# Sample attention of a decoder step: keys of two pairs before values of two pairs, values in 64-column tiles, probability copies moved between engines

## What is computed

```
comp  = compressed blocks of the past                     # 32 of them
p_c   = softmax(q @ comp.K - slope * distance)            # importance of blocks
idx   = top 16 blocks by sum of p_c over the group's heads
o_s   = softmax(q @ K[idx] - slope * distance) @ V[idx]   # selected branch
o_w   = softmax(q @ Kwin  - slope * distance) @ Vwin      # window of 512
o     = gate0 * p_c @ comp.V + gate1 * o_s + gate2 * o_w
```

## Time and profile before

| what | value |
|---|---|
| median of three runs | 909.55 us |
| the profiled execution's own time | 906.55 us |
| span of that execution | 904.7 us |
| sample stage in the span | 310.4 to 417.4 us |
| TensorE busy over the span | 826.2 us (91%) |
| VectorE, ScalarE, GpSimd busy | 418.0, 335.7, 135.0 us |
| mean granted TensorE clock | 0.96 of full speed |

### The profile page before, as it was taken

How to read it: one execution, slowest core, us unless ns; L and a number is a source line. 1 busy time by engine, 2 the same in 40 slices (tenths; PEclk the granted TensorE clock), 3 DMA queues, 4 the chain that set the end, 5 groups by cost and what they waited for, 6 DMA issues and landing times.

```text
span 904.7 us, 18157 instructions
## 1 busy us (share of the span) xinstructions
PE 826.2 (91%) x7775; PEld 752.2 (83%) x7775; DVE 418.0 (46%) x782; ACT 335.7 (37%) x626; POOL 135.0 (15%) x160
## 2 busy tenths in 40 slices
PE   5999998997888867785999999999999999999995
PEld 4999977775555645465999999999999999999995
DVE  5435646664555475565327433344233433243432
ACT  6511155552566565463225431133212331043311
POOL 0001101100785345530220000000000000000120
PEclk9999999998899889896999999999999999999998
DMA  8912628842461206526221122222221122222002
GB/s 299 323 72 95 192 70 248 259 168 93 134 206 36 83 1 233 190 79 178 94 93 50 48 89 93 93 93 93 93 86 41 59 93 93 94 93 93 1 1 105
DMA packets 48794, 103.03 MB, mean 114 GB/s; under 512 B 7499, under 2 KB 19167, under 8 KB 46430
## 3 DMA queue, kind: packets, MB, share of 16 engines
q1 hardware_dynamic: 41821, 68.61, 23.1%
q0 software_dynamic: 6912, 33.56, 10.9%
HBM read 97.75 MB, written 8.53 MB: 117 GB/s over the span
## 4 chain that ended last, share of the span: by engine, by line
PE 52%; DVE 1%; ACT 0%; DVEq 0%; issue 0%
PE banks L2003 51%; PE banks L2044 0%; DVE y L1993 0%; PE banks L2070 0%; DVE wl L1923 0%; PE banks L2060 0%; ACT wh L1867 0%; DVE hT L1936 0%; DVE hT L1961 0%; DVE xl L1940 0%; ACT low L1881 0%; DVE xl L1929 0%; ACT xh L1883 0%; DVEq L1816 0%; ACT small L1911 0%
## 5 line engine op out<-in xcount | busy, mean ns | idle before, releaser
L2003 PE MATMUL banks<-xh,wh 128*128 128x288 f32 x640 | 138.3, 298 | 4.3 <-DVE xl L1929 3.9
L2003 PE MATMUL banks<-xl,wh 128*128 128x288 f32 x640 | 138.1, 297 | 0.0
L2003 PE MATMUL banks<-xh,wl 128*128 128x288 f32 x640 | 137.7, 297 | 0.0
L1867 ACT ACTIVATE wh<-low 128x1024 fp32r<-128x1024 f32 x72 | 75.0, 1050 | 103.1 <-PE banks L2003 102.9
L2003 PE MATMUL banks<-ah,wh 128*128 128x288 f32 x512 | 110.2, 297 | 0.0
L2003 PE MATMUL banks<-al,wh 128*128 128x288 f32 x512 | 109.6, 296 | 0.0
L2003 PE MATMUL banks<-ah,wl 128*128 128x288 f32 x512 | 109.6, 296 | 0.0
L2003 PEld LDWEIGHTS banks<-xh,wh 128*128 128x128 f32 x640 | 104.0, 190 | 5.0 <-DVE wl L1923 4.2
L2003 PEld LDWEIGHTS banks<-xl,wh 128*128 128x128 f32 x640 | 104.1, 190 | 0.0
L2003 PEld LDWEIGHTS banks<-xh,wl 128*128 128x128 f32 x640 | 104.0, 190 | 0.0
L1961 DVE TENSOR_TENSOR hT<-banks,hT 128x288 f32<-128x288 f32 x64 | 26.3, 453 | 138.9 <-PE banks L2003 138.9
(11 more groups left out here) (340 smaller groups left out, 1372.3 us busy)
## 6 DMA issues: line engine op xcount, KB each, us to landing
low<-in_w_up SPq DMA_DIRECT2D x8, 2048.0 KB, 8.2
low<-in_w_down SPq DMA_DIRECT2D x8, 2048.0 KB, 7.7
zone<-in_cmp_w SPq DMA_DIRECT2D x16, 256.0 KB
o_swin<-in_state_win SPq DMA_DIRECT2D x8, 504.0 KB
px<-in_x_prompt SPq DMA_DIRECT2D x4, 512.0 KB, 5.3
u_raw<-in_w_in SPq DMA_DIRECT2D x1, 2048.0 KB, 10.0
q_raw<-in_w_in SPq DMA_DIRECT2D x1, 2048.0 KB, 10.4
low<-in_state_win SPq DMA_DIRECT2D x4, 512.0 KB
```

The lines of the kernel that those rows point to most:

```text
L1867: act.activation(wcols(m.wh, i), raw_cols(i), ACT.Copy).then_inc(wh_ready, 1)
L2003: last = pe.matmul(out(i, hf), w[wi], half(x[:, k, :], hf), start=first and part == 0, stop=end and part == 2)
```

## The change

- TensorE's program becomes phases of two pairs: K0 K1 V0 V1 K2 K3 V2 V3. V1 and K2 change places. `turn_output` of a pair b-1 stands behind K(b), with `small_scores` waiting for one more stored output (`o_kept`).
- `values` uses two matmuls a position tile instead of four: 64 probability columns of one e (both groups) stationary, 128 value columns of both groups moving. Half of the results (probabilities of one group with values of the other) are computed and not used. The merge reads the full 128 columns.
- For pairs 0 and 2 ScalarE copies all six units of turned probabilities; for pairs 1 and 3 the split of three and three stays.
- ScalarE's queue: `exponents(b)` stands behind `keep_keys` of units 0 to 3 of pair b+1; `exponents(b+1)` stands behind all six copies of pair b.
- VectorE's queue: scores of b, scores of b+1, merge of b, its copies of b+1, merge of b+1.
- GpSimd issues all page loads of pair 2, then all of pair 3, in a row behind the bias of pair 1, each waiting for the unit whose slot it fills.

The diff, cut to its core:

```diff
+    COPIER = [(("act",) * VN, ("act",) * 3 + ("dve",) * 3)[n % 2] for n in range(NPAIR)]
+    def keep_probs(eng, n, i):
+        eng.wait_ge(p_turned, VN * n + i + 1)
+        if VN * n + i >= 3:
+            eng.wait_ge(v_done, VN * n + i - 2)
...
-                if 1 <= n < NPAIR - 1:
-                    for i, x in enumerate(ORDER):
+                if n == 1:
+                    for b in range(2):
+                        for i, x in enumerate(ORDER):
+                            if x < 4:
+                                pool.wait_ge(v_done, VN * b + i + 1)
+                                for e in range(2):
+                                    load_pages(pool, m, b + 2, e, x, sems)
...
+            for b in range(0, NPAIR, 2):
+                for u in range(3):
+                    pack(act, b, u)
+                keys_of(b, 0, UN)
+                if b:
+                    keep_output(b - 1)
+                for u in range(3):
+                    pack(act, b + 1, u)
+                keys_of(b + 1, 0, 4)
+                exponents(b)
+                keys_of(b + 1, 4, UN)
+                for i in range(VN):
+                    keep_probs(act, b, i)
+                exponents(b + 1)
+                for i in range(VN):
+                    if COPIER[b + 1][i] == "act":
+                        keep_probs(act, b + 1, i)
+                keep_output(b)
...
+            for b in range(0, NPAIR, 2):
+                scores_of(b)
+                scores_of(b + 1)
+                merge(b)
+                for i in range(VN):
+                    if COPIER[b + 1][i] == "dve":
+                        keep_probs(dve, b + 1, i)
+                merge(b + 1)
...
             def small_scores(n):
-                if n >= 3:
-                    pe.wait_ge(o_kept, n - 2)
+                if n >= 2:
+                    pe.wait_ge(o_kept, n - 1)
...
+                out = lambda e, r: pb[4][64 * e:64 * e + 64, P * r:P * r + P]
                 for mm in range(QUAD if i < X else 0):
-                    for e, g in tiles:
+                    for e in range(2):
+                        last = pe.matmul(out(e, int(ORDER[i] == 4)).rearrange("p (g d) -> p g d", g=NKV),
+                                         m.spT[i % 3][:, P * mm + 64 * e:P * mm + 64 * e + 64],
+                                         m.slot[2 * (n % 2) + e][:, ORDER[i], mm, :]
+                                         .rearrange("p (g k) -> p g k", g=NKV)[:, :, HD:2 * HD],
+                                         start=(i == 0 and mm == 0), stop=False, skip_group_check=True)
...
+            for b in range(0, NPAIR, 2):
+                keys_of(b)
+                if b:
+                    pe.wait_ge(sel_step, b * SEL_STEPS + 1)
+                    turn_output(b - 1)
+                keys_of(b + 1)
+                values_of(b)
+                values_of(b + 1)
             turn_output(NPAIR - 1)
```

More of the change, by code:

```diff
@@ L1511, in _, with keys_of @@
-            for n in range(NPAIR - 2, NPAIR):
-                keep_output(n)
+            def keys_of(n, first, last):
+                for u in range(first, last):
+                    if u == 1:
+                        act.wait_ge(c_step, n * C_STEPS + 2)
+                        act.activation(m.sp[n % 2][:, CMP0:CMP0 + NBLK], m.sp[n % 2][:, CMP0:CMP0 + NBLK], ACT.Exp,
+                                       bias=cneg, accum_out=csum).then_inc(c_exp, 1)
+                    keep_keys(n, u)
+                    if u + 3 < UN and PACKER[u + 3] == "act":
+                        pack(act, n, u + 3)
@@ L1514, in _ @@
+            keep_output(NPAIR - 1)
         @block.vector
@@ L1662, in turn_keys @@
                     pe.wait_ge(k_kept, n * UN + u - 1)
-                if n >= 2 and u < 2:
-                    pe.wait_ge(pt_dve, 3 * (n - 1))
+                if n == 2 and u < 2:
+                    pe.wait_ge(*copied(1, u + VN - 2))
                 for mm in range(QUAD):
@@ new lines, in values, with keys_of @@
+                last.then_inc(v_done, 1)
+            def keys_of(n):
+                small_scores(n)
+                for i in range(X + 1):
+                    if i < X:
+                        turn_keys(n, 2 * i)
+                        turn_keys(n, 2 * i + 1)
+                    if i == 1:
+                        pe.wait_ge(p_cmp, n + 1)
+                        pe.matmul(pb[5][:, IMP:IMP + NBLK], const(m, "headsum"), m.sp[n % 2][:, CMP0:CMP0 + NBLK],
+                                  start=True, stop=True).then_inc(imp_mm, 1)
+                    if i in (2, 4, X):
+                        scores(n, TOGETHER[(i - 1) // 2])
@@ new lines, in values_of @@
+            def values_of(n):
+                for i in range(VN + 1):
+                    if i < VN:
+                        turn_probs(n, i)
+                    if i >= 1:
+                        values(n, i - 1)
+                    if i == 1 and n % 2:
+                        turn_output(n - 1)
+            for b in range(0, NPAIR, 2):
[6 more added lines that the diff above has]
+                values_of(b + 1)
```

165 lines of the change are left out of this document (46 added, 119 removed).

## The result

The changed kernel takes 910.28 us (median of 20 runs, 906.66 to 916.89), the kernel before, run beside it, 906.41 us (902.99 to 910.10). The ratio is 1.0042, with a 95% interval of 1.0025 to 1.0060: 3.9 us slower, where 0.65 us faster was forecast. The profiled execution of after takes 906.66 us with a span of 904.8 us, nearly the same as before's. That hides the difference: it is the fastest of after's 20, while before's profiled 906.55 us is close to its median, and K0 starts at 310.04 us in it and at 312.21 in before's, behind a part of the program that the change does not touch. From K0's first matmul to the MLP's first matmul before takes 108.4 us and after 111.2. I call this stretch the stage from here on and compare kernels by it.

A forecast was written before the change was run, and what follows sets the result against it. The sample stage's end sets the time, with TensorE pauses beside full DMA engines. Stalls 12.0 to 1.0 us, K1 -0.7, K2 -0.8, values +5.1, exponents +3.6, K3 +3.0: 0.7 sooner, 909.55 to 908.9 us; range 903.0 to 920.5.

The forecast's parts named there:

- the one for K2: K2 after V1 resembles K0's 11.9 us, with pages landed and no low clock; 12.5 with the uncovered merge.
- the part on the stalls: Values phases: fewer TensorE records beside full DMA engines, so stalls fall from 12.0 to 1.0 us, all in V1.
- Rival A: Pauses belong to full DMA engines, not TensorE's instruction count; V0, V1, V3 lose 11.0 us more, 919.9 us; chance 0.26.
- V1's stall of 1.0 us: V1, lying wholly in the load of pairs 2 and 3, loses 1.0 us; V0 and V3 lose none.
- The unit at 1.02 us: Values phases: a new unit of 16 records takes 1.02 us, 0.43 more than the old unit of 32.
- The last unit: End of each values phase: 12 records for 24 take 0.8 us.
- The queue's change: K1: ScalarE's exponents moved behind units 0 to 3 let unit 6 start sooner; 0.7 us off, 17.6.
- K3's wait for VectorE: K3, with no values phase ahead, waits about 4 us for a VectorE pack; K3 grows by 3.0 us.
- The wait for pair 1's output: Ahead of K3's small scores: some 1.1 us for the stored output, hidden under the longer VectorE wait.
- Rival B: The MLP starts at full clock, worth about 2.8 us; 905.1 without V1's stall, 903.5 with more off K1, K3; chance 0.17.
- C: Values matmuls: the two 64-column tiles do not run at the same time; 18 to 20 us more, 928; chance 0.05.
- The forecast's case: Whole kernel: no change that can be told, within 0.5%, 905.0 to 914.1 us; chance of same 0.53.

The follow-up runs named there:

- after_no_load3: The changed kernel without pair 3's page and window loads, pair 3 working on pair 1's rows; ratio to before 1.0004.
- paced: exp_early with last_grouped's last values unit, and pair 3's loads issued in steps from GpSimd's queue during K2; ratio to before 0.9976.
- order_only: The changed kernel with the 32-column values matmuls and merge of the kernel before; ratio to before 1.0006.
- exp_early: The changed kernel with VectorE copying units 3 to 5 of every pair and ScalarE's next exponents behind its first three copies; ratio to before 1.0069.
- last_grouped: The changed kernel with the last values unit's matmuls ordered by their rows, so that the two sequences alternate; ratio to before 1.0039.
- spread2: spread with pair 3's tile 2 issued earlier, in K2, and its tile 3 behind K3's first GpSimd pack; ratio to before 0.9908, 900.01 us.
- after_spread: The changed kernel with only its page and window loads timed as in spread2; ratio to before 1.0016.
- tiles_only: The kernel before, in its own order, with only the 64-column values matmuls of the change; ratio to before 1.0037.
- spread: The changed kernel with 32-column values for pairs 0 to 2, last unit grouped in pair 3, exp_early's copies and exponents, page loads spread out; ratio to before 0.9920.
- before_no_load2: The kernel before without pair 2's page and window loads, pair 2 working on pair 0's rows; ratio to before 0.9922.

## Why the prediction was wrong

Each phase from its start to the next, forecast against the profile of after: K0 11.9 and 12.4; K1 17.6 and 17.4; V0 with the exponents 11.3 and 11.4; V1 10.7 and 11.0; K2 12.5 and 15.9; K3 17.0 and 15.8; V2 with the exponents 11.3 and 11.1; V3 9.7 and 10.7; the tail 2.5 and 2.4. The sum is 3.5 us above the forecast, and K2+K3 make 2.2 of it, V3 with its last unit 1.0, K0 0.5. That is after's fastest execution; its median one is 3.6 us longer, and no profile shows where. The forecast time, 908.9 us, lies 1.4 us from the measured 910.28 only by luck: it was set on the median of three runs, 909.55, which over 20 runs is 906.41.

**The failed step is the one for K2**: "its pages have been there for some microseconds ... It resembles K0". Its own pages had landed. But the part on the stalls had itself put pairs 2 and 3 together at 26 us of load from 347, which is 373: nine microseconds into the forecast's K2. I had used that for V1's stall and not for K2. VectorE starts pair 2's scores 4.54 us behind V1's end where the step had 1.3, and K3 ends 11.5 us behind the end of VectorE's sums (382.37), for the forecast's 11.9. So K2+K3 is long by VectorE's late start, 3.2 us, less 0.6 because its chain took 15.7 us for 16.3 and 0.4 at K3's end. after_no_load3 gave the forecast's figure back, 1.20 us, and so did paced, 1.22, where no load ran at that point. The step's other premise, that TensorE does not start K2 at the lower clock, failed with it: the granted clock was 0.50 from 366 to 368 us.

**Rival A, and what it missed.** The pauses do need DMA engines at work: without its load V0 took 7.4 us with the same instructions. I gave this rival 0.26. But "not the number of TensorE's instructions" was wrong, for with half of them V0 and V3 lost nothing (119 and 118 records at full clock) where order_only had pauses. And its price was wrong: it let V0, V1 and V3 lose what they had lost before, 11 us, while the loss of 3 to 4 us stood in K2. "The need falls from well over what a full DMA lets through to about that" held for TensorE's own instructions alone; the signals to VectorE and ScalarE, late in the earlier trace rows, do not get fewer with wider tiles. V1's stall of 1.0 us came as 0.56 us, and it was the wait for pair 0's merge (see exp_early), a term that the sum does not have.

**The values.** The unit at 1.02 us was right. The last unit was taken at 0.8 by its record count; it took 1.9, with three changes between 32 and 64 rows and one sequence after the other; which of the two costs it, no run tells apart. V0 and V2 hid that under the exponents, so they came out at 11.4 and 11.1 against 11.3, and with a wait of 0.81 and 0.53 for 1.8. That the two phases came out right is luck: TensorE's work was 1.1 us too short in the forecast, and ScalarE's exponents, which end when they were forecast to, covered the error. V3 shows it in full, and last_grouped halved the unit.

**K1.** The queue's change did what was forecast: unit 6's transposes start 12.6 to 12.8 us into K1 in all nine kernels with after's ScalarE order; the forecast had 12.75, before had 13.4. But only after and paced kept the gain in their profiles (17.4 and 17.6). In the other seven kernels with that order the same 16 transposes behind it run at the low clock, as in order_only (TensorE's timeline and the window):

```profile
334.94 3.96 PE L1681 MATMUL banks<-consts,zone 128*128 128x128 f32 x16 [0.75 <-ACT zone L1482]
```

```profile
334.90:340.70 5.80, 5.76 (x41) 3.45 (x41) 4.73 (x9) 3.19 (x6) 2.65 (x3) 0.66 0.00 0
```

K1 is 18.4 or 18.5 us there, for 18.3 in before: the 0.7 us are given back by a clock that comes back later. In after's profile that stretch was granted 1.00 and took 4.8 us. How often after itself keeps it, one profile doesn't tell.

**K3 and the output.** K3's wait for VectorE came (2.62 us, with one more of 0.92; the profile names ScalarE's copy, which stands behind its wait for VectorE's small scores). The wait for pair 1's output was to lie under it. It does not; it stands ahead of it, 0.96 us from 377.11 to 378.07, and 2.1 to 2.3 us of idle time in paced, spread2 and after_spread, where pair 3's loads were still running and ScalarE took the transpose 1.5 to 1.7 us late.

**The MLP's start.** Rival B did not come: its first matmul waits 3.90 us as before and runs at the low clock. C was excluded by the unit of 1.02 us. The forecast's case, no difference by 0.5%, is the one that the measured 0.42% falls in, but the sign is the other one, and the interval excludes what was forecast.

## What to carry to other kernels

When a stretch has its DMA engines full, don't price only the phase in which the load is issued: follow the load to its last byte, and ask which engine's queue is critical there, for the signals between engines are late as long as it lasts. Fewer and larger instructions move that cost. Loads issued at intervals were in the two fastest complete kernels, but with early exponents and other copies beside them: from order_only's 1.0006 to spread2's 0.9908 all of these changed, and the loads alone, in after, gave 0.0026 within overlapping intervals. The issues themselves take time in GpSimd's queue, so look for what stands behind them. When an order brings two phases together, ask which wait the phase between them had covered, here the merge. And a doubled instruction is a loss that pauses can hide: price it in the state the kernel would have without them.

## What the runs showed of the hardware

- Beside full DMA engines signals come late, as well as TensorE's next instructions: VectorE's merge started 1.65 us (after) and 4.8 us (tiles_only) behind the matmuls it waits for, 0.16 us in after_no_load3 (368.46 to 368.62). At a mean share of 0.87 (spread) TensorE ran 216 records in 8.3 us with no such pause, at 0.74 (spread2) it had one of 1.87 us. In after two signals of TensorE, whose matmuls end 1.9 us apart, are recorded 0.12 us apart, just when TensorE itself goes on (363.60 to 363.74). By what path a data transfer holds these up is not shown by any run, nor do the runs part the page transfers from GpSimd's issuing of them.
- GpSimd's page issues took 0.94 us each and began 1.24 us apart (after, 345.75 to 349.48). Four of them ahead of a pack cost TensorE 3.28 us (spread), four ahead of the bias VectorE 2.35 us (spread2).
- The Trainium skill (Runtime: NRT & Kernel Launch, Instruction fetch mechanics) says that instruction blocks are fetched by DMA while the former one runs, and that this is mostly hidden. The pause of 3.87 us in V3, gone when the weights' load was moved away, is what one would see if it is not hidden beside a full DMA. The DMA record of the trace counts instruction transfers by a kind of their own, 16 KB each on queue 8, without naming the engine that they serve. The window of the pause, 409.7 to 413.6, has one, from 410.79 to 411.84, and the like pause of before_no_load2 has one too. TensorE goes on only 1.75 us after the first has ended. But V1 of after has one (356.95 to 357.93, DMA share 1.03) with no pause, and the pauses at K2's start in after and tiles_only have none. So that a late fetch is part of V3's pause is argued, not shown, and such a transfer is not what made the others. The DMA view's line for the window of that pause (packets, MB, share):

```profile
q8 instruction: 1, 0.02, 1.7%
```

- The order of matmuls with 32 and 64 rows within one unit changed its length from 1.9 to 0.95 us, at the same 12 records.
- TensorE ran at a granted clock of 0.57 for 4 us in last_grouped's V3, behind a wait of 1.45 us, and K1's last transposes ran at some 0.65 or at 1.00 for the same code. Such luck moved single stages by a microsecond or two, as much as most terms of the sum.
